# Two small tiles moved ahead of the large regions in on-chip memory

## The reference

```python
h = rmsnorm(x, norm_mix)
z, xbc, dt, lru_y, lru_x, q, k, v, ret_g, gate_pre = split(h @ w_in)
y_ssd = ssd_mixer(z, xbc, dt, ...)        # chunks of 128, decay = exp(differences of a running sum)
y_lru = rglru_mixer(lru_y, lru_x, ...)
y_ret = retention_mixer(q, k, v, ret_g)
x = x + sum(sigmoid(gates) * (branches @ w_branch)) @ w_o
x = x + (gelu(conv(a)) * u) @ w_out       # a, u = split(rmsnorm(x) @ ffn_w_in)
x = rmsnorm(x)
for layer in range(2):                    # second block
    x = x + 0.5 * swiglu(rms_norm(x), w13, w2)
    y = short_conv_mixer(h) if layer == 0 else causal_mla_attention(...)
    x = x + concat(y, memory_attention(...)) @ w_out
    x = x + 0.5 * swiglu(rms_norm(x), w13, w2)
```

## The kernel before

| tile | bytes of a partition | begins at byte | past a multiple of 64 / of 2,048 |
|---|---|---|---|
| `raw`, `w_hi`, `w_lo`, `h_hi`, `h_lo`, `x`, `stage`, `tmp` | 94,208 together | 16,512 | 0 / 128, each of them |
| `cpad` (the data begin 16 bytes in) | 4,128 | 110,720 | 0 / 128 |
| `acc` | 2,048 | 114,848 | 32 / 160 |
| `rstd` | 2,048 | 116,896 | 32 / 160 |
| `vec` | 1,464 | 118,944 | 32 / 160 |
| `mats` (seven 128x128 matrices) | 3,584 | 120,416 | 32 / 1,632 |
| `neg_r` | 1,024 | 124,000 | 32 / 1,120 |
| `fill` (used by nothing) | 32 | 125,024 | 32 / 96 |
| the two regions | 98,304 | 125,056 | 0 / 128 |
| `spare` | 4,096 | 223,360 | 0 / 128 |
| `ident_r` | 512 | 227,456 | 0 / 128 |
| `small` | 656 | 227,968 | 0 / 640 |

## Time and profile before

### The profile page before, as it was taken

How to read it: one execution, slowest core, us unless ns; L and a number is a source line. 1 busy time by engine, 2 the same in 40 slices (tenths; PEclk the granted TensorE clock), 3 DMA queues, 4 the chain that set the end, 5 groups by cost and what they waited for, 6 DMA issues and landing times.

```text
span 3247.7 us, 37188 instructions
## 1 busy us (share of the span) xinstructions
PE 3149.3 (97%) x13833; PEld 2519.8 (78%) x13833; DVE 1852.6 (57%) x2389; ACT 923.2 (28%) x1243; POOL 347.1 (11%) x160
## 2 busy tenths in 40 slices
PE   7889999999999999999998999999999999999999
PEld 5768567877888887888877788887888877488887
DVE  8896445437776655554576755445454446464542
ACT  2443233324322222222222322222222234332222
POOL 2334124022000000000033000002000022000000
PEclk9999899999999999999999999999999998999999
DMA  3222012322322222222332222222223321022232
GB/s 125 84 72 97 26 39 91 117 72 72 117 91 97 97 98 91 91 97 97 108 107 78 78 97 97 97 104 96 96 93 104 104 82 46 1 97 97 97 104 90
DMA packets 79372, 287.67 MB, mean 89 GB/s; under 512 B 9056, under 2 KB 9312, under 8 KB 78880
## 3 DMA queue, kind: packets, MB, share of 16 engines
q1 hardware_dynamic: 77328, 278.03, 24.6%
q0 software_dynamic: 1936, 8.13, 0.7%
HBM read 284.02 MB, written 2.10 MB: 88 GB/s over the span
## 4 chain that ended last, share of the span: by engine, by line
PE 76%; issue 14%; POOL 5%; DVE 4%; ACT 1%; DMA 0%; POOLq 0%; DVEq 0%; ACTq 0%
PE ps L590 23%; PE ps L592 23%; PE ps L591 23%; POOL w_lo L544 5%; PE ps L683 1%; PE ps L1067 1%; PE ps L699 1%; PE ps L928 1%; PE ps L749 1%; PE ps L1066 0%; PE ps L1073 0%; DVE rstd L1567 0%; ACT w_hi L1111 0%; DVE w_lo L1503 0%; PE ps L934 0%
## 5 line engine op out<-in xcount | busy, mean ns | idle before, releaser
L590 PE MATMUL ps<-h_hi,w_hi 128*128 128x512 f32 (+1 forms) x2443 | 964.7, 395 | 36.5 <-POOL w_lo L544 24.1
L592 PE MATMUL ps<-h_hi,w_lo 128*128 128x512 f32 (+1 forms) x2443 | 953.4, 390 | 0.0
L591 PE MATMUL ps<-h_lo,w_hi 128*128 128x512 f32 (+1 forms) x2443 | 953.1, 390 | 0.0
L1111 ACT ACTIVATE w_hi<-raw 128x1024 fp32r<-128x1024 f32 x525 | 555.3, 1058 | 1301.1 <-PE ps L592 1281.9
L1503 DVE TENSOR_TENSOR w_lo<-raw,w_hi 128x1024 fp32r<-128x1024 f32 x390 | 476.9, 1223 | 432.8 <-ACT w_hi L1111 432.3
L590 PEld LDWEIGHTS ps<-h_hi,w_hi 128*128 128x128 f32 x2443 | 463.0, 190 | 144.3 <-POOL w_lo L544 23.5
L591 PEld LDWEIGHTS ps<-h_lo,w_hi 128*128 128x128 f32 x2443 | 463.1, 190 | 96.0 <-issue 2.7
L592 PEld LDWEIGHTS ps<-h_hi,w_lo 128*128 128x128 f32 x2443 | 462.1, 189 | 96.1
L590 PE MATMUL ps<-mid_hi,w_hi 128*128 128x512 f32 x1208 | 471.5, 390 | 2.2 <-DVE mid_lo L1578 2.1
L591 PE MATMUL ps<-mid_lo,w_hi 128*128 128x512 f32 x1208 | 470.4, 389 | 0.0
L592 PE MATMUL ps<-mid_hi,w_lo 128*128 128x512 f32 x1208 | 470.4, 389 | 0.0
(11 more groups left out here) (363 smaller groups left out, 2679.7 us busy)
## 6 DMA issues: line engine op xcount, KB each, us to landing
raw<-in_wstream SPq DMA_DIRECT2D x525, 512.0 KB, 3.2
x<-in_x SPq DMA_DIRECT2D x8, 256.0 KB, 5.8
x_in<-in_x POOLq DMA_DIRECT2D x8, 256.0 KB, 2.9
mem_x<-in_mem POOLq DMA_DIRECT2D x2, 1024.0 KB, 5.2
out<-x POOLq DMA_DIRECT2D x8, 256.0 KB, 3.4
tmp<-in_ret_decay POOLq DMA_DIRECT2D x1, 1024.0 KB, 5.2
rope_r<-in_rope_r POOLq DMA_DIRECT2D x1, 512.0 KB, 3.7
mats<-in_mats SPq DMA_DIRECT2D x1, 320.0 KB, 6.7
```

The costliest lines, as they stand in the source:

```text
L590: nc.tensor.matmul(dst, hi_w, hi_x, start=first, stop=False)
L591: nc.tensor.matmul(dst, hi_w, lo_x, start=False, stop=False)
L592: return nc.tensor.matmul(dst, lo_w, hi_x, start=False, stop=last)
L1111: nc.scalar.activation(w_hi[:, n % HL], raw[:, r], ACT.Copy).then_inc(hi_ready, 1)
```

## The change

`ident_r` and `small` are declared outside the `with` blocks, ahead of the regions: `ident_r` before `neg_r`, and `small` in place of `fill`. Nothing else differs; no instruction is added, removed or moved.

```diff
         mats = sb(ctx, "mats", [P, len(MATS), P])
+        ident_r = sb(ctx, "ident_r", [P, P], F32R)
         neg_r = sb(ctx, "neg_r", [P, 2, P], F32R)
-        sb(ctx, "fill", [P, 8])
+        small = sb(ctx, "small", [P, 164])
         mat = {name: mats[:, j] for j, name in enumerate(MATS)}
...
             spare = sb(one, "spare", [P, 2, S])
-            ident_r = sb(one, "ident_r", [P, P], F32R)
-            small = sb(one, "small", [P, 164])
```

## The result

The changed kernel takes 3280.28 us at the median (3278.44 to 3286.96, four runs) against 3255.24 for the kernel before (3249.5 to 3258.26, four runs): 25 us more, a ratio of 1.0084, 95% interval 1.007 to 1.0098. Of the changed kernel nine executions are recorded, with a median of 3281.72. No change was forecast, and the range ended at 3264.

What follows compares the result with a forecast made beforehand. TensorE, busy with matmuls for 97% of the span, was taken as the bound. All terms were 0, leaving the profiled 3249.5 us; the median, 6.1 us above, gave 3255.6 us, range 3246 to 3264.

Steps and rivals of the forecast that it cites:

- Products on moved tiles: Three split-product lines: 5,040 matmuls with moved moving operands keep their pace; 0 us, bound 5 us down or up.
- two residues in place of one: Matmuls on moved tiles slow beside VectorE or ScalarE writes as tile offsets differ: 15 us, 3271 us, chance 0.06.
- 439 or fewer matmuls in 100 us on `mid_hi` and still 443 on `h_hi`: Feed-forward stretches: profile sign for the slower rival of differing tile offsets, chance 0.06; no change meant 443 on both.
- No wait appeared: Tile lifetimes: waits are written by hand, so moving `ident_r` and `small` adds or removes none; 0 us.
- `ident_r` and `small` cost nothing by themselves: Loads of `ident_r`, accesses to `small`: 0 us, bounds 3 us each; rival that only they slow, 3262 us, chance 0.03.
- VectorE's, ScalarE's and GpSimd's busy times: VectorE and ScalarE work on large tiles: unaffected by the 1,152-byte move and mostly hidden behind matmuls; 0 us.
- the transfers to `raw` and `x_in`: Panels go to unmoved `raw`, `x_in` pieces into moved tiles by GpSimd's queue; transfers cost 0 us.
- `mem_x` still takes 5.2 us: Transfer that GpSimd's `w_lo` waits 5.1 us for: its median stays near 5.2 us.
- the 5 us of the products: Bound on 5,040 matmuls with moved operands in the three split-product lines: 1 ns each, down or up.

Runs made afterwards that it cites:

- the kernel of TensorE alone: Separate kernel without the computation, each product on its own line: plain fp32 takes 592 ns at distances 0 and 128; 256 columns 283 and 281 ns.
- the sweep: Separate kernel with only TensorE's product triple, moving operand's start stepped against the weights: 226.7 ns from start to start at multiples of 256 bytes, 233.4 at 128.
- 64 bytes: Kernel before with `fill` 64 bytes wider, so the regions and what lies behind move up by 64 bytes: 3259.03 us, ratio 1.001.
- 128 bytes: Kernel before with `fill` 128 bytes wider, so the regions and what lies behind move up by 128 bytes: 3283.85 us, ratio 1.0091.

## Why the prediction was wrong

**The step that failed** is "Products on moved tiles": "From each length to the next it is 105 or 106 ns for 128 columns, so the beginning adds nothing above 1 ns. I take 0. The bound is that 1 ns either way". It measured 6.2 ns for each product, 31 us for 5,040, where the bound was 5 us. The mechanism of the sum was right, that a change of addresses can act through the pace of the matmuls; the term was mis-sized, at nothing. Two things were wrong in it.

First, the rows were of another kind of product. Lines 716, 761 and 796 are plain fp32 products, which with 512 columns start every 429 ns; the three lines multiply rounded fp32 and start every 227 ns, reading the same bytes in about half the time. The trace calls both f32, but their durations, 592 and 389 ns for the same shape, tell them apart. The changed kernel still has 592 and 379 ns in those rows, and the kernel of TensorE alone has 592 ns at both distances: they can't show what the faster products feel. Second, those that could show it all stood in step. The prediction saw that both `h_hi` and `mid_hi` "begin 128 past a multiple of 2,048" and looked for other offsets of the moving operand, taken by itself. It never set it against the stationary operand, which is read at the same time. There was no row in the kernel before in which one of these products was out of step by 128 bytes, so the honest bound was far wider than 1 ns.

**The rival that came nearest** was "two residues in place of one": slower by 15 us with a chance of 0.06, decided from 2 ns on. Its direction, its place (`mid_hi`, not `h_hi`) and its sign in the profile, "439 or fewer matmuls in 100 us on `mid_hi` and still 443 on `h_hi`", are what came: 432 and 443. Its mechanism was not: it blamed writes of VectorE and ScalarE beside the read. Its price was luck, too: the 3 ns between 389 on `mid_hi` and 392 on `h_hi` come from products at half the clock, and at full clock both started every 227 ns. The kernel moved as a whole but for the weights keeps all those distances and loses 62 us, and the sweep has the loss with all other engines still.

**What was right.** No wait appeared; `ident_r` and `small` cost nothing by themselves (0.9998 with the regions in step); VectorE's, ScalarE's and GpSimd's busy times are the same within 2 us, and the transfers to `raw` and `x_in` within 0.1 us; `mem_x` still takes 5.2 us. The range was a little narrower than its own bounds: with the 5 us of the products it ends near 3244 below, and still at 3263 above.

**The cause, as far as it is shown.** TensorE loads the weights of the next product while it multiplies (in the kernel of TensorE alone the load starts within 4 ns of the product, and 188 of the 227 ns are its). When rounded-fp32 tiles lie a multiple of 256 bytes apart, a product of 128 rows, 128 columns of weights and 512 moving columns starts every 226.7 ns, and at the other distances tried every 229.1 to 238.0. Distance and not address (every tile moved: no loss), weights and not other tiles (all but the weights moved: loss on all products), TensorE alone (the sweep). That it is the two reads which meet in memory is the nearest reading of this, but no run looks inside. For these products the loss is up to 11 ns in 227 (4 bytes past a multiple of 256); plain fp32 and bf16 show none, with 429 and 215.8 ns from start to start at all the distances tried.

**What stays open.** Why a moved `w_lo` slows the product that it is for as well as the one beside its load, and the exact shape within 256 bytes: both may hang on timing, as the loads of 64 columns suggest, but no theory of mine forecast those rows. Open is also why the granted clock differs between the kernels, which matters in the next paragraph.

**Where the kernels' loss differs from the sum of the products.** The change costs 25 us against 31, moving all but the weights 62 against 77 (12,369 x 6.2), and 64 bytes 4 against 12, but 128 bytes 30 against 31. Two things account for most of it. Fewer products count: those of 256 columns lose nothing (283 ns long at 0 and 281 at 128), and at a granted clock of 0.50 a product starts every 427 ns in step (69 on `h_hi` and `h_lo` before) and out of step (107 of them with all but the weights moved). At full clock, starts lie 6.1 ns further apart on the moved tiles of the changed kernel, 30 us over some 4,880 products; with all but the weights moved it is 5.7 ns on `h_hi` and `h_lo` and 6.1 on the others, 69 us over some 11,900. And the granted clock isn't the same in all: the 51 runs of the kernel before that stand beside the experiments take 3247.58 to 3248.29 us at a mean clock of 0.983 and 3253.27 to 3258.64 at 0.979, 2.5 us for each 0.001 by a straight line through them. By that line, which makes these estimates, the losses at equal clock are 28 us for the change, 31 for 128 bytes, 11 for 64 bytes, 66 for all but the weights and 50 for `w_lo` alone. What the waits give back is small; TensorE's wait for `w_lo` ahead of the first product on `h_hi` falls from 24.1 us to 20.8:

```profile
L589 PE MATMUL ps<-h_hi,w_hi 128*128 128x512 f32 x2411 | 957.5, 397 | 33.8 <-POOL w_lo L543 20.8 <-ACT tmp L1114 7.5 <-DVE w_lo L1502 2.9
```

## What to carry to other kernels

Where TensorE is the bound with rounded-fp32 products of 128 weight columns and 512 moving ones, keep each moving tile a multiple of 256 bytes from the weight tiles (226.7 ns from start to start here, against 229.1 to 238.0 at the other distances tried), and after any change of declarations work out these distances again; here 128 unused bytes behind `small` keep the change and lose nothing (1.0002). To judge the size of a mechanism by a small loss, compare runs at the same granted clock: 64 bytes cost 4 us by the medians and some 11 at equal clock. A bound from "similar" rows is worth only as much as the similarity: same type, same rate, and both operands of an instruction, not one. Where all rows of a kind share one alignment, the trace has nothing to say about another, and a small kernel with one engine at work gives the whole curve in one run, at least for one shape.

## What the runs showed of the hardware that was not expected

- The distance between moving and weight tiles counts for rounded fp32 with 128 weight columns and 512 moving ones: 226.7 ns from start to start at a multiple of 256 bytes, 229.1 at 64 past, 233.1 to 234.1 at the other multiples of 32, and 238.0, 233.3 and 231.7 at 4, 8 and 16 bytes past.
- Plain fp32 (429 ns from start to start, at 0 and 128 bytes) and bf16 (215.8 ns, at 0, 64 and 128) don't feel it; nor do 256 moving columns of rounded fp32 (283 and 281 ns long), nor the same products at a granted clock of 0.50 (427 ns from start to start, in step and 128 bytes out of step).
- bf16 is 11 ns faster from start to start than rounded fp32 in step, at the same 512 columns.
- With weights of 64 columns no distance tried was at 389 ns for all three products: 390 to 394 at 0 and 391 to 392 at 128.
